# The outgoing products of a state space scan, four tiles at a time in four column groups, with two product buffers and another order of work on TensorE

## The reference

```python
bu_re = jnp.einsum('blgh,gph->blgp', ug, bb_re)
bu_im = jnp.einsum('blgh,gph->blgp', ug, bb_im)
_, _, h_re, h_im = lax.associative_scan(_complex_affine_combine, (lr, li, bu_re, bu_im), axis=1)
y = (jnp.einsum('blgp,ghp->blgh', h_re, c_re.astype(f32))
     - jnp.einsum('blgp,ghp->blgh', h_im, c_im.astype(f32)))
y = y.reshape(Bsz, L, D_SSM) + d.astype(f32) * u
y = jax.nn.gelu(y)
zg = y @ glu_w.astype(f32) + glu_b.astype(f32)
```

## Time and profile before

| | |
|---|---|
| three runs | 1379.47, 1383.82 and 1384.68 us, median 1383.82 |
| the profiled execution | 1379.36 us, of which the span is 1377.6 us |
| TensorE (matmuls) busy | 1180.9 us, 86% |
| VectorE, ScalarE, GpSimd busy | 412.0, 206.9 and 121.4 us (30%, 15%, 9%) |
| the chain that ended last | TensorE 61%, DMA 30%, VectorE 5%, ScalarE 2% |
| DMA | 377.31 MB, mean 274 GB/s |

### The profile page before, as it was taken

The page is one execution under the profiler, slowest core; times in us unless marked ns, Lnnn a source line. Parts: engine busy times, 40 slices in busy tenths (PEclk is TensorE's granted clock), DMA queues, the critical chain, the costliest instruction groups (busy, mean ns, idle before and its releaser), DMA issues.

```text
span 1377.6 us, 18774 instructions
## 1 busy us (share of the span) xinstructions
PE 1180.9 (86%) x8146; PEld 642.3 (47%) x8146; DVE 412.0 (30%) x812; ACT 206.9 (15%) x389; POOL 121.4 (9%) x148
## 2 busy tenths in 40 slices
PE   6989997986667767666999999999799879999996
PEld 5745455532222222222545547888676443333332
DVE  4265733110001001000256385422464331111113
ACT  3112421010000000000000031111321132112111
POOL 0010000000005870000044200000000000000000
PEclk9999998998889789888999999999999989999999
DMA  8432739999999999999714431312313629999991
GB/s 290 162 110 75 305 124 400 430 427 425 428 428 425 428 429 426 426 430 423 291 31 157 164 137 62 123 36 91 122 61 127 283 87 408 423 421 422 421 422 73
DMA packets 62397, 377.31 MB, mean 274 GB/s; under 512 B 6129, under 2 KB 7537, under 8 KB 37105
## 3 DMA queue, kind: packets, MB, share of 16 engines
q1 hardware_dynamic: 60736, 369.64, 65.9%
q10 hardware_dynamic: 1584, 6.55, 1.3%
HBM read 375.13 MB, written 1.05 MB: 273 GB/s over the span
## 4 chain that ended last, share of the span: by engine, by line
PE 61%; DMA 30%; DVE 5%; ACT 2%; issue 1%; POOL 0%; SPq 0%; DVEq 0%; ACTq 0%
DMA arena<-in_w_expert_up 22%; PE psum L468 10%; PE psum L471 9%; PE psum L2636 6%; DMA arena<-in_expert_w_up 5%; PE psum L1298 3%; PE psum L2144 3%; PE psum L763 3%; PE psum L2660 3%; DMA arena<-in_w_expert_gate 3%; PE psum L2247 2%; PE psum L2671 2%; PE psum L1904 2%; PE psum L1010 2%; PE psum L1328 2%; PE psum L1092 1%
## 5 line engine op out<-in xcount | busy, mean ns | idle before, releaser
L1298 PE MATMUL psum<-arena 128*32 128x256 f32 x2048 | 151.0, 445 | 95.1 <-DMA arena<-in_w_expert_up 56.8
L468 PE MATMUL psum<-arena 128*128 128x512 f32 x352 | 160.1, 604 | 2.9 <-ACT arena L507 1.6
L1298 PEld LDWEIGHTS psum<-arena 128*32 128x32 f32 x2048 | 70.7, 124 | 176.7 <-DMA arena<-in_w_expert_up 73.4
L1328 PE MATMUL psum<-arena 128*32 128x512 f32 x512 | 123.9, 635 | 15.6 <-DMA arena<-in_w_expert_down 10.3
L471 PE MATMUL psum<-arena 128*128 128x256 f32 x544 | 123.6, 382 | 3.0 <-ACT arena L1732 2.0
L2636 PE MATMUL psum<-arena 128*64 128x512 f32 x512 | 116.0, 595 | 2.1 <-DMA arena<-in_expert_w_up 2.1
L471 PEld LDWEIGHTS psum<-arena 128*128 128x128 f32 x544 | 101.4, 189 | 20.2 <-issue 5.6
L468 PEld LDWEIGHTS psum<-arena 128*128 128x128 f32 x352 | 65.0, 191 | 81.6 <-issue 81.3
L1328 PEld LDWEIGHTS psum<-arena 128*32 128x32 f32 x512 | 31.4, 116 | 95.8 <-issue 69.9
L1359 DVE TENSOR_TENSOR arena<-arena,psum 128x256 f32<-128x256 f32 x16 | 6.8, 422 | 224.0 <-ACT arena L1342 224.0
L2636 PEld LDWEIGHTS psum<-arena 128*64 128x64 f32 x512 | 35.8, 137 | 69.3 <-issue 68.9
(11 more groups left out here) (464 smaller groups left out, 1285.7 us busy)
## 6 DMA issues: line engine op xcount, KB each, us to landing
arena<-in_w_expert_gate SPq DMA_DIRECT2D x32, 2048.0 KB, 25.3
arena<-in_w_expert_up SPq DMA_DIRECT2D x32, 2048.0 KB, 26.3
arena<-in_w_expert_down SPq DMA_DIRECT2D x31, 2048.0 KB, 24.4
arena<-in_w_in SPq DMA_DIRECT2D x21, 2048.0 KB, 8.8
arena<-in_expert_w_gate SPq DMA_DIRECT2D x32, 1024.0 KB, 11.5
arena<-in_expert_w_up SPq DMA_DIRECT2D x32, 1024.0 KB, 13.6
arena<-in_expert_w_down SPq DMA_DIRECT2D x32, 1024.0 KB, 10.2
arena<-in_w_out SPq DMA_DIRECT2D x4, 2048.0 KB, 8.0
```

Of the source, the lines that this page charges most:

```text
L468: mm = pe.matmul(o, lhs[:, k, sub * P:(sub + 1) * P], w[:, k, :], start=(k == 0), stop=(k == kt - 1))
L1298: mm = pe.matmul(ps[32 * c:32 * c + 32], xin[:, e, k], w[:, j, 256 * n:256 * n + 256], start=(k == 0), stop=(k == KD - 1))
L1328: mm = pe.matmul(y_ps[at:at + 32, 512 * n:512 * n + 512], hid_T4[:, j, half], w[:, j, 512 * n:512 * n + 512], start=(half == 0 and j == 0) ...
```

## The change

- `emit` works on four tiles at once, `emit(q)` for q = 0 to 3, in four column groups; it waits for the products of two steps.
- GpSimd's products go to two buffers, `prs[s % 2]`. The second lies in the part of the ring that later holds gates. The products of step `s` wait for the emission of steps up to `s - 2`, that is `ssm_emitted` at `s // 2`.
- There is a `yield` between the turning of B and the first `drive`, and the string is a new one: two steps of `a` or `c` behind nearly every `drive`.
- `c` has 9 steps in place of 5, so the string behind it has 4 fewer left. Unit 6 and 7 of the weights are exchanged to fit (the second attention unit ahead of the GLU's), and ScalarE takes three filler jobs out ahead of the GELU in place of one.

```diff
-        b2 += [column_unit(D["w_in_2"], 1536, 256), column_unit(D["w_in_2"], OFF_MOBA, 512), column_unit(D["ssm_glu_w_2"], 0, 1024)]
-        b2 += [column_unit(D["w_in_2"], OFF_MOBA + 512 * j, 512) for j in range(1, 3)]
+        b2 += [column_unit(D["w_in_2"], 1536, 256), *(column_unit(D["w_in_2"], OFF_MOBA + 512 * j, 512) for j in range(2))]
+        b2 += [column_unit(D["ssm_glu_w_2"], 0, 1024), column_unit(D["w_in_2"], OFF_MOBA + 1024, 512)]
...
-            pr = cols.take("ssm_p", 2048, top=True).rearrange("p (r s) -> p r s", r=4)
+            prs = [a.rearrange("p (r s) -> p r s", r=4) for a in (cols.take("ssm_p", 2048, top=True), half_ring[:, 10240:12288])]
...
                     mm.then_inc(inc("ssm_b_turned"), 1)
+                yield
                 pe.wait_ge(*count("ssm_bT", 1))
...
-                def emit(s):
-                    pe.wait_ge(*count("ssm_products", s + 1))
-                    q = s // 2
-                    if s % 2 == 0 and q >= 2:
+                def emit(q):
+                    pe.wait_ge(*count("ssm_products", 2 * q + 2))
+                    if q >= 2:
                         pe.wait_ge(*count("ssm_y", q - 1))
                     for n, c in enumerate((c_re, nc_re, nc_im, nc_im)):
-                        for i in range(2):
-                            tile = 2 * s + i
-                            o = bank(4 + q % 2)[32 * (tile % 4):32 * (tile % 4) + 32, 0:SEQ]
-                            mm = pe.matmul(o, c[:, 32 * tile:32 * tile + 32], pr[:, n, i * SEQ:(i + 1) * SEQ],
+                        for i in range(4):
+                            tile = 4 * q + i
+                            o = bank(4 + q % 2)[32 * i:32 * i + 32, 0:SEQ]
+                            mm = pe.matmul(o, c[:, 32 * tile:32 * tile + 32],
+                                           prs[i // 2][:, n, (i % 2) * SEQ:(i % 2 + 1) * SEQ],
                                            start=(n == 0), stop=(n == 3))
...
-                drive(0)
-                yield
                 for s in range(HB):
-                    if s + 1 < HB:
-                        drive(s + 1)
-                    yield
-                    emit(s)
+                    drive(s)
                     yield
+                    if s and s % 2 == 0:
+                        emit(s // 2 - 1)
+                        yield
+                emit(3)
+                yield
...
-                    x = xs[s % 2]
+                    x, pr = xs[s % 2], prs[s % 2]
                     pool.wait_ge(*count("ssm_scanned", s + 1))
-                    if s >= 1:
-                        pool.wait_ge(*count("ssm_emitted", s))
+                    if s >= 2:
+                        pool.wait_ge(*count("ssm_emitted", s // 2))
...
-            take_turns(pe, "baaba" + "ab" * 11 + "bcb" + "cc" + "bb" + "cc", a=proj_rkv.parts[0], b=ssm_scan.parts[0],
-                       c=lambda pe: (next(beside_rwkv) for _ in range(5)))
+            take_turns(pe, "abab" + "aabaabaa" + "bbaabaa" + "bbaabcc" + "bb" + "cccc" + "b" + "ccc", a=proj_rkv.parts[0],
+                       b=ssm_scan.parts[0], c=lambda pe: (next(beside_rwkv) for _ in range(9)))
...
-            next(copies_beside)
+            for _ in range(3):
+                next(copies_beside)
```

More of the change, by code:

```diff
@@ L334, in two_blocks @@
         b2 += [column_unit(D["w_out_2"], 512 * j, 512) for j in range(2)]
-        U_SSM, U_RWKV, U_LORA, U_GLU, U_GATE, U_UP, U_OUT2 = (U_B2 + x for x in (0, 1, 4, 6, 9, 15, 18))
-        U_MOBA = [U_B2 + x for x in (5, 7, 8)]
+        U_SSM, U_RWKV, U_LORA, U_GLU, U_GATE, U_UP, U_OUT2 = (U_B2 + x for x in (0, 1, 4, 7, 9, 15, 18))
+        U_MOBA = [U_B2 + x for x in (5, 6, 8)]
         U_END = U_B2 + len(b2)
```

4 lines of the change are left out of this document (2 added, 2 removed), and 2 rows, old and new, of the table SHARED.

## The result

The changed kernel takes 1369.33 us, median of six runs (1368.05 to 1371.00); the kernel before takes 1381.40, median of six (1379.05 to 1384.68). The ratio is 0.9913, with a 95% interval of 0.9897 to 0.9929. The profiled execution took 1368.05 (span 1366.2), against 1379.36 (span 1377.6). The medians are 12.1 us apart.

The account below looks back on a forecast made before the run. TensorE was taken to bound the stage from `proj_u` to `glu_proj`; the terms there and in RWKV-7 sum to -13.1 us, giving 1370.7 from the median of 1383.82. Its own range was 1364 to 1375, for all 1363.5 to 1378.5.

Parts of the forecast that it names:

- emissions: Scan on TensorE: four emissions of 1.85 us in four column groups replace eight of 1.85; -7.4 us.
- gaps around the turned B: TensorE ahead of the first `drive`: filler steps cover two copies, so waits of 0.78 and 1.32 go; -2.1 us.
- cold pair: Two filler steps behind those gaps, at a lowered clock: 7.13 us in place of 8.54; -1.4 us.
- wait for GpSimd: TensorE's wait at 761.03 for GpSimd's last multiplication in the scan goes; -1.4 us.
- filler blocks in the scan: Projection steps between scan work: 23 in 11 blocks in place of 19 in 15; +12.9 us.
- P to G, all five: TensorE from the start of `proj_u` (P) to that of `glu_proj` (G), five scan terms together; +0.6 us.
- the switch in RWKV-7: Change from `proj_qkv2` to `proj_gates_tail` inside a filler pair: the second step waits for ScalarE; +1.0 us.
- F to A: From the first filler of RWKV-7's last stretch (F) to second attention's first L590 (A), shorter; -14.7 us.
- Rival 1: Scan emissions: four column groups don't run together, so emissions keep their cost; 1378.1 us, chance 7%.
- Rival 2: Scan: the four emissions wait for GpSimd, 4 to 8 us in all; 1375 to 1379 us, chance 12%.
- Rival 3: Scan: GpSimd stretches VectorE's scans too, emissions wait some 5 us each; slower, 1396 us, chance 3%.
- Rival 4: RWKV-7: neither the switch pair nor L1969 waits; 2.5 us less, 1368.2; chance 78% together with the forecast.

Follow-up runs that it names:

- experiment 1: Changed kernel with each emission's 16 matmuls issued as two halves of 8, two column groups at a time; 1373.69 us.
- experiment 2: Changed kernel with each emission's 16 matmuls issued tile by tile, four per column group in a row; 1381.66 us in one run.
- two-buffer kernel: Kernel before with only a second GpSimd product buffer and the wait for an emission one step later; 1382.61 us, again 1378.89.
- Experiment 10: Changed kernel with three more GpSimd multiplications per step, results overwritten, placed beside VectorE's scans; 1392.07 us in one run.
- experiment 6: Changed kernel with 5 filler steps in the scan in place of 9, old load order, one copy ahead of the GELU; 1380.01 us.

## Why the prediction came out right

The forecast was 1370.7 and the time is 1369.33. The sum was -13.1, and P to A is 13.14 shorter. The forecast stood on a median of 1383.82 from three runs; over six it is 1381.40, so the medians differ by 12.1, 1.0 less than the sum. From 1381.40 the same sum gives 1368.3, which is 1.0 low where the forecast on record is 1.4 high. By its own steps, with the same sign convention:

| step | forecast | measured | from |
|---|---|---|---|
| emissions | -7.4 | -7.3 | 4 x 1.87 less 8 x 1.85 |
| gaps around the turned B | -2.1 | -2.0 | `proj_u` to its successor 14.34 in place of 14.81, the turning 0.88 in place of 2.38 |
| cold pair | -1.4 | -1.65 | the pair 7.06 in place of 8.48, the `drive` ahead of it 1.07 in place of 1.30 |
| wait for GpSimd | -1.4 | -1.4 | no idle time ahead of any L1614 |
| filler blocks in the scan | +12.9 | +12.6 | 81.1 less 68.4 by the starts of the rows, the cold pair taken at 7.06; it is also what is left of P to G |
| P to G, all five | +0.6 | +0.25 | 112.27 less 112.02 |
| the switch in RWKV-7 | +1.0 | +1.4, again +1.1 | 184.03 and 183.74 less 182.66 |
| F to A | -14.7 | -14.8 | 21.41 less 36.17 |

**The emissions** were right, and for the reason given: L1298 and L1328 foretold them. Rival 1 is out: an emission takes 1.87, not 3.7. The rule that stood against it (the Trainium skill, "TensorE: Matmul & The Clock Gate", Part 3, a weight load overlaps a running matmul only where the row group differs) isn't borne out here: sixteen matmuls, all on the same rows, each with its own weights, take 1.87, and one after the other they would take some 7.1; the first emission's loads, 32 records with 1.45 busy, begin with it at 714.66 and lie inside it. What the argument lacked is that the order of issue decides (experiments 1 and 2). L1298 writes its groups in turn, the changed kernel does too, and so the carry-over held; had the emission gone tile by tile, the same rows would have foretold the wrong number. That the order was the same was luck as far as the argument goes: the prediction notes it and makes no condition of it.

**The clock** is the term whose size held and whose reason did not. I tied the fall of the clock to the two gaps. The two-buffer kernel has the gaps and no fall, twice. That the changed kernel loses the cold pair is seen in both its traces, but since it has the second buffer too, that closing the gaps did it isn't shown. As far as the runs show, the -1.4 came out by luck.

**GpSimd and VectorE.** Products were forecast for 711.7, 729.9, 748.1 and 765.9; GpSimd's last multiplications end at 711.41, 730.68, 748.79 and 766.72, while the emissions start at 714.66, 732.78, 751.19 and 768.04. The cover is 3.2, 2.1, 2.4 and 1.3, more than the 1.8, 1.7, 1.9 and 1.1 between my two rows. `proj_u` starts 1.29 later in this trace than in the one I counted on; with that taken off the emissions are within 0.25 of the forecast, and the products are 0.5 to 1.6 early, since I had given every rotation and every step's products the worst price seen. Rival 2 didn't occur. Its mechanism is there: VectorE's addition or subtraction is longer in seven of the eight rotations, up to 1.75, and GpSimd's last multiplication in five of the eight steps, 1.71 to 1.72, which are the amounts of the earlier trace rows. Timelines of VectorE and of GpSimd in the changed kernel, one step:

```profile
719.51 0.68 DVE L1653 TENSOR_TENSOR arena<-psum,arena 128x512 f32<-128x512 f32 x1
720.23 0.82 DVE L1655 TENSOR_TENSOR arena<-arena 128x512 f32<-128x512 f32 x1
720.97 1.75 DVE L1656 TENSOR_TENSOR arena<-arena 128x512 f32<-128x512 f32 x1
722.76 2.44 DVE L1661 TENSOR_TENSOR_SCAN arena<-arena 128x256 f32<-128x256 f32 x4
```

```profile
719.23 1.27 POOL L1691 TENSOR_TENSOR arena<-arena 128x512 f32<-128x512 f32 x1
720.46 1.71 POOL L1692 TENSOR_TENSOR arena<-arena 128x512 f32<-128x512 f32 x1
```

Only the addition, the subtraction and the one multiplication beside them are longer; L1650 to L1653, which read PSUM, and the scans, which come when GpSimd is done, are not. Rival 3, the slower kernel, is the case in which the scans are stretched as well. Experiment 10 puts GpSimd beside them: a step's four take 5.2 in the mean and 6.5 at most where I gave 5.4, and the kernel is slower than before, 1392.07 against the 1396 of that rival, though with work added that the rival doesn't have. So its mechanism is real, and its low chance rested on the right row.

**The switch in RWKV-7** was placed right and a little short: the wait is 0.98, and the two steps, now two blocks, cost 0.22 more to start. I had counted block starts in the scan and not here. The 0.3 between the two traces (+1.4, +1.1) is the idle stretch put down to issue, 1.21 in one and 0.95 in the other.

**The end of RWKV-7** was right in every row: one 1.02 left, 1.56 for VectorE (forecast 1.5), and 4.07 ahead of L590 where I had 4.2. Rival 4 is out, as both of the waits it left out are there.

**Nothing waits on loads**, as forecast: no row between P and A has idle time that a DMA ended.

## What to carry to other kernels

Where matmuls with 32 columns of weights share the array, change the column group at every matmul: the same sixteen took 1.87, 2.75 or 4.53 us by their order alone. Once TensorE no longer bounds a stage, matmuls saved there turn into waits unless work from a later stage is moved in (without it 10.1 of the 13.1 us were gone here). Look at the place that the work is taken from for a wait that it was covering (1.56 here). Judge a change of under 1% by distances between fixed rows of the trace, since a stretch that no edit touches moved by 3 us between two traces of one kernel. Even such distances move, by 1 to 1.6 us where the clock falls in one trace and not in another, so look at the rows inside them too.

## What the runs showed of the hardware

**VectorE and GpSimd take turns by whole instructions** when both read two operands from SBUF: an addition or subtraction of 0.68 takes up to 1.75 and a multiplication of 1.26 takes 1.71, a scan of 0.61 takes 1.62. In the rows above, the multiplication L1692 ends at 722.17, 1.12 behind the end of L1655 (721.05), and L1656, begun at 720.97, ends at 722.72, 0.55 behind that: each takes about its own time once the other is through. VectorE's multiplications that read one operand from PSUM stay at 0.68 beside the same work of GpSimd. Which operands are shared agrees with the Trainium skill, "GPSIMD Engine Reference", 1. Specifications; how much it costs is this trace's.

**At a change of column group about two matmuls are hidden**, 0.87 and 0.95 us, where each group's four matmuls (or each pair of groups' eight) come in a row; the 0.87 rests on the 7.13 of matmuls with 128 columns of weights. Where the group changes at every matmul sixteen take 1.87.

**Equal gaps, unequal clock.** Behind 0.78 and 1.32 us of idle time the granted clock fell to 0.59 over four microseconds in one kernel, in both traces, and stayed at 1.00 in another whose TensorE rows up to there are the same, in both traces. Another place is in RWKV-7: behind a wait of 1.73 or 1.74 the rows up to the next filler take 8.2 in twelve of the fourteen traces, with the clock down to about 0.5, and 6.6 in the other two (experiments 6 and 10), with the clock at 1.00. The changed kernel and experiment 6:

```profile
849.98 5.85 PE L1890 MATMUL psum<-arena 64*64 64x128 f32 x122 [1.73 <-DVE arena L2039]
```

```profile
846.98 4.26 PE L1890 MATMUL psum<-arena 64*64 64x128 f32 x122 [1.73 <-DVE arena L2039]
```

Behind a wait of 4.07 it was low in both traces of the kernel before and in both of the changed one, and the stretch behind it varied from 6.02 to 7.15.
